# Empty slots of a gathered key list: from row 0 to an index above the gather's bound

## What is computed

```python
def select_keys(scores, q_pos, n_sel):                       # n_sel = 256
    scores = jnp.where(k_pos[None, None, :] <= q_pos[None, :, None], scores, -jnp.inf)
    return lax.top_k(scores, n_sel)[1].astype(jnp.int32)

def sample_attention(q, k_new, v_new, qi, ki_new, wi, cache_k, cache_v, cache_kidx, page_table, rel_bias):
    ...
    idx = select_keys(indexer_scores(qi, wi, ki_all), q_pos, n_sel)
    ...
    def gather(cache, new):
        return jnp.where(in_past[..., None, None], cache[phys, off], gather_rows(new, nidx))
    return sparse_attend(q, gather(cache_k, k_new), gather(cache_v, v_new), q_pos, idx, rel_bias)
```

## Time and profile before

| | |
|---|---|
| median of 3 runs | 1870.47 us (1870.22 to 1871.6) |
| profiled execution, its own time | 1877.6 us |
| span of the profile | 1875.6 us |
| PE, DVE, ACT, POOL busy | 92%, 46%, 35%, 35% |
| DMA packets, bytes | 69477, 158.56 MB |
| gathers of K and V | 256, from 503.4 to 964.1 us |

### The profile page before, as it was taken

How to read it: one execution, slowest core, us unless ns; L and a number is a source line. 1 busy time by engine, 2 the same in 40 slices (tenths; PEclk the granted TensorE clock), 3 DMA queues, 4 the chain that set the end, 5 groups by cost and what they waited for, 6 DMA issues and landing times.

```text
span 1875.6 us, 28975 instructions
## 1 busy us (share of the span) xinstructions
PE 1727.2 (92%) x11176; PEld 1411.4 (75%) x11176; DVE 857.6 (46%) x1809; ACT 653.2 (35%) x1370; POOL 655.2 (35%) x745
## 2 busy tenths in 40 slices
PE   7888999899966787888889999999999999999998
PEld 6553464699944455555555689999999999999997
DVE  4572889277843445666441343313232323232324
ACT  4464787666122333343231022222222121212123
POOL 1100336788554656655513140404040404040300
PEclk9799999999987889999899999999999999999999
DMA  8301202111185656555572001111010102020202
GB/s 241 93 1 48 93 36 77 49 35 42 35 267 147 174 168 180 161 155 157 148 254 81 1 1 45 46 38 53 30 59 22 68 13 76 7 83 2 99 1 96
DMA packets 69477, 158.56 MB, mean 85 GB/s; under 512 B 9402, under 2 KB 26030, under 8 KB 69120
## 3 DMA queue, kind: packets, MB, share of 16 engines
q1 hardware_dynamic: 48000, 85.43, 13.7%
q0 software_dynamic: 21376, 71.75, 12.9%
HBM read 144.40 MB, written 12.76 MB: 84 GB/s over the span
## 4 chain that ended last, share of the span: by engine, by line
PE 82%; DVE 7%; issue 4%; POOL 3%; another core or an unknown queue 2%; ACT 2%; DMA 1%; SPq 0%; DVEq 0%; POOLq 0%; ACTq 0%
PE psum L1841 7%; PE psum L1839 7%; PE psum L1828 7%; PE psum L1827 7%; PE psum L1829 7%; PE psum L1840 7%; PE psum L1768 6%; PE psum L1549 4%; PE psum L1385 3%; PE psum L1398 3%; PE psum L1574 2%; PE psum L1663 2%; PE psum L1685 2%; PE psum L1365 2%
## 5 line engine op out<-in xcount | busy, mean ns | idle before, releaser
L1827 PE MATMUL psum<-n_hi,wup_hi 128*128 128x384 f32 (+1 forms) x768 | 251.3, 327 | 0.0
L1839 PE MATMUL psum<-h_hi,wdn_hi 128*128 128x384 f32 (+1 forms) x768 | 250.9, 327 | 0.0
L1828 PE MATMUL psum<-n_lo,wup_hi 128*128 128x384 f32 (+1 forms) x768 | 250.8, 327 | 0.0
L1829 PE MATMUL psum<-n_hi,wup_lo 128*128 128x384 f32 (+1 forms) x768 | 250.8, 327 | 0.0
L1841 PE MATMUL psum<-h_hi,wdn_lo 128*128 128x384 f32 (+1 forms) x768 | 250.2, 326 | 0.0
L1840 PE MATMUL psum<-h_lo,wdn_hi 128*128 128x384 f32 (+1 forms) x768 | 250.1, 326 | 0.0
L2437 DVE TENSOR_TENSOR h_lo<-h_full,h_hi 128x384 fp32r<-128x384 f32 (+1 forms) x96 | 112.0, 1178 | 262.0 <-ACT h_hi L1246 253.4
L1238 ACT ACTIVATE hrelu<-psum 128x384 f32<-128x384 f32 (+1 forms) x96 | 45.4, 473 | 501.9 <-PE psum L1829 501.9
L932 POOL TENSOR_TENSOR wup_lo<-wup_full,wup_hi 128x4096 fp32r<-128x4096 f32 x8 | 72.3, 9034 | 420.4 <-ACT wup_hi L1222 420.4
L2442 DVE TENSOR_TENSOR x_region<-psum,x_region 128x384 f32<-128x384 f32 (+1 forms) x192 | 102.8, 535 | 252.9 <-PE psum L1841 251.8
L1100 ACT ACTIVATE arena<-x_region,arena 128x384 bf16<-128x384 f32 (+2 forms) x192 | 166.5, 870 | 29.8 <-POOL arena L864 29.8
(11 more groups left out here) (328 smaller groups left out, 3202.0 us busy)
## 6 DMA issues: line engine op xcount, KB each, us to landing
wup_full<-in_w_up SPq DMA_DIRECT2D x8, 2048.0 KB, 8.0
wdn_full<-in_w_down SPq DMA_DIRECT2D x8, 2048.0 KB, 7.7
arena<-in_x_prompt SPq DMA_DIRECT2D x16, 512.0 KB, 9.4
arena<-in_w_in SPq DMA_DIRECT2D x3, 2048.0 KB, 8.4
arena<-in_w_in SPq DMA_DIRECT2D x12, 512.0 KB, 5.7
out<-arena SPq DMA_DIRECT2D x17, 256.0 KB, 4.5
arena<-in_w_out SPq DMA_DIRECT2D x8, 512.0 KB, 9.4
out<-arena SPq DMA_DIRECT2D x8, 512.0 KB, 2.7
```

The lines of the kernel that those rows point to most:

```text
L1827: pe.matmul(b, wu_hi[:, k, col], n_hi[:, k, o:o + w], start=(k == 0), stop=False)
L1828: pe.matmul(b, wu_hi[:, k, col], n_lo[:, k, o:o + w], start=False, stop=False)
L1829: i = pe.matmul(b, wu_lo[:, k, col], n_hi[:, k, o:o + w], start=False, stop=(k == KT - 1))
L1839: pe.matmul(b, wd_hi[:, f, col], h_hi[:, hf, 0:w], start=(f == 0), stop=False)
```

## The change

Every gather of K and V gets a bound, the last row of the cache (40959), and `oob_is_err=False`: a place whose index is above it is passed over, and nothing is copied for it. `slot_lists()` adds 2^20 to the row number of each place that no query wants, so that empty places have such an index. What stays in the ring's empty places is what lay there before; the masks are as they were.

```diff
@@ slot_rows (POOL)
                     pool.indirect_dma_start(ring[:, r % 4, kk, :], None, src,
-                                            bass.IndirectOffsetOnAxis(ap=slotidx[:, c:c + 1], axis=0)).then_inc(ring_in[r % 4], 16)
+                                            bass.IndirectOffsetOnAxis(ap=slotidx[:, c:c + 1], axis=0),
+                                            bounds_check=ck.shape[0] - 1, oob_is_err=False).then_inc(ring_in[r % 4], 16)
@@ slot_lists (VectorE)
-                link(dve.scalar_tensor_tensor(out=sl, in0=bits_[:, 0:128].rearrange("p (b l) -> p b l", b=DB), scalar=256.0,
+                empty, row = (x[:, 0:128].rearrange("p (b l) -> p b l", b=DB) for x in (posi_, hi_))
+                dve.tensor_scalar(empty, got[:, :, 2, :], 0.0, float(1 << 20), ALU.is_equal, ALU.mult)
+                link(dve.scalar_tensor_tensor(out=row, in0=bits_[:, 0:128].rearrange("p (b l) -> p b l", b=DB), scalar=256.0,
                                               in1=got[:, :, 1, :], op0=ALU.mult, op1=ALU.add))
+                link(dve.tensor_tensor(sl, row, empty, ALU.add))
```

## The result

The changed kernel takes 1883.03 us, median of 5 runs (1881.84 to 1888.82), against 1870.54 us for the kernel before (5 runs, 1870.22 to 1871.6). The ratio is 1.0077 [1.0062, 1.0092], so it is slower by 12.5 us. Of these 12.5 us the two profiled executions show only 4.8: that of before was itself 7 us above its median (1877.6 us), that of after is within 1 us of its own (1882.42 us).

The account below looks back on a forecast made before the run. TensorE was busy 92% of the span; in the gathers' stage POOL, not the bytes, set the gathers' pace. Terms -1 + 0.6 + 0.8 = +0.4 us on 1870.47 gave about 1871 us, range 1860 to 1905 us.

Parts of the forecast that it names:

- no change: Whole kernel: the likeliest case, about 1871 us, with 1867 to 1874 us as its range; chance 0.34.
- the smallest difference that can be told: Whole kernel: 0.2%, 3.7 us, taken as about what a measurement can tell from none.
- Bytes: Gathers of K and V: 15.6 MB fall away, worth -1 us, bounds 0 and -3.
- VectorE: Building of the slot list: two more instructions on the path, +0.5 to +0.6 us, taken as +0.6.
- POOL's work in a gather: POOL's time per gather with a bound: taken as 0 us more, range -0.09 to +0.95 us a gather.
- dear end: POOL's gathers: at +0.95 us each, 1973 us or more; a skill-page estimate of 1.3 us a gather would exceed that.
- slower rival: POOL's gathers: dropping rows one by one spends 0.4 us a gather again, about 20 us, 1890 us; chance 0.33.
- the sum's own rule: Gathers' stage: only the 27 gathers under the chain's unattributed pieces, 34 us, count as on the path.
- The register: POOL, ahead of each gather: a 29 ns bound load, 27 on the path, +0.8 us; 7.4 us without cover.
- faster rival: Gathers' stage: TensorE's stalls come from the gathers' traffic and fall with it, about 1863 us; chance 0.30.
- mark: TensorE's "issue" waits in the gathers' stage: near 36 us instead of 47 would show that traffic causes the stalls.

Follow-up runs that it names:

- e3: The changed kernel with the bound at 0, so nearly all rows are passed over; 1789.31 us against 1790.05 for the kernel before, ratio 0.9988.
- e1: The kernel before with only the bound on every gather, all bytes moved; 1791.89 us against 1790.05, ratio 1.0018.
- e6: The kernel before with only the bound on every gather, timed again at the 1871 level; 1885.14 us against 1872.0, ratio 1.0076.
- e5: The changed kernel as it is, timed again at the 1871 level; 1881.12 us against 1872.0 for the kernel before, ratio 1.006.
- e7: The kernel before with 112 rows per gather instead of 128 once the ring is filled, no bound; 1878.4 us against 1872.0, ratio 1.0042.
- e8: The changed kernel with the bound loaded into a register once instead of 256 times; 1871.62 us against 1872.0 for the kernel before, ratio 1.0003.
- e10: The kernel before with the bound from one register loaded once, no VectorE edit, all bytes moved; 1794.61 us against 1788.76, ratio 1.0034.
- e12: The changed kernel with one register load and an empty instruction ahead of each gather; 1874.67 us against 1871.15 for the kernel before, ratio 1.0021.

## Why the prediction was right or wrong

The time lies in the range of 1860 to 1905 us, but that was luck: the range reached beyond 1874 us for a rival, rows handled one by one, that the runs show not to exist. The case that was forecast, no change, is not what happened: the kernel is slower by more than three times what was called the smallest difference that can be told.

*Bytes.* The working gave 15.6 MB, and 15.57 are gone. Their worth was put at -1 us, bounds 0 and -3. The runs agree with a small gain: at the 1790 level all of the gathers' bytes are worth 3 to 5 us (e3 against e1), of which 23%, an estimate in proportion, would be about 1 us. At the 1871 level the bound with all bytes (e6, +13.1 us) and with the 15.6 MB saved (e5, +9.1 us) differ by 4 us, no more than an edit can cost there without adding work (e7). The sentence that the transfers are hidden under POOL's pace held in the main. The Trainium skill, "DMA: Bandwidth & Descriptors", section "The descriptor swizzle", gave 0 for this term; the runs can't tell 0 from 1 us, and they show no partition's engine.

*VectorE.* +0.6 us stood in the sum; two runs give -0.4 and +1.8 us, both within their error of it. The trace of after shows 0.3 us. The term was small and is small.

*POOL's work in a gather.* Taken at 0, with -0.09 to +0.95 us as bounds; it is +0.053 to +0.056 us. The reason given for 0, that the indices are read and turned into addresses either way, was too simple; the reason against a dear end held. The price is the same with no row above the bound (e1), with a quarter (e5), and with nearly all (e3), so the slower rival's mechanism, a second handling row by row, does not exist here. Nor does the dear end that came by the Trainium skill, "GPSIMD Engine Reference", section "Elementwise — side-by-side cycle accounting": 12 cycles an element gave an estimate of 1.3 us a gather, and the runs show 0.05. By the sum's own rule 27 gathers on the path at 0.056 us would be 1.5 us. At the 1871 level e8 shows 0 [-2, +3 us] for it, VectorE's edit and the saved bytes together; its own price there was not measured, and if the 4 us between e5 and e6 are the bytes' worth, it is about as much. At the 1790 level, where POOL has 7% of the chain, e1 and e10 show 2 to 6 us.

*The register: the step that failed.* The prediction put it at +0.8 us, "On the path are the gathers under the unattributed pieces", 27 of them at 29 ns. The duration was right and the pause even hides it. But undoing this one part (e8) takes the change from 1.006 to 1.0003, 9.5 us, and what replaces it in time without being a load (e12) gives back 3.5 us. So at this level a term that was worked out as duration times count was mis-sized by more than ten times, and by its own duration, all 256 on the path, it could be 7.4 us at most. What shows in the profile instead is not POOL: the three profiles with the loads at this level (the change, e5, e6) have 4 to 5% of the chain unattributed and TensorE idle for 102 to 108 us, the four without (before, e7, e8, e12) 1 to 2% and 93 to 95 us. At the 1790 level the loads show no price (e1 against e10), and one and the same kernel, the bound alone, loses 1.8 us there (e1) and 13.1 us here (e6).

*The faster rival and its mark.* It said that TensorE's stalls fall with the bytes, and its mark, "issue" near 36 us, came true in the first profile: 35 us. The time rose all the same, for waits under other names grew by more, those for copies that themselves wait for an unnamed releaser. Nor does the mark go with the bytes: the second profile of the changed kernel has 43.8 us, and the bound alone, with all bytes moved, 38.2. The mark was badly chosen: TensorE's whole idle time in the stage is the thing to compare, and it grew by 7 us, from 94.7 to 101.7.

*What stays open.* Why a register load ahead of each gather lengthens TensorE's stalls, while an instruction of the same length does so less, or not at all; and what these stalls are. All that is shown is that they are in the gathers' stage, that other engines' copies start several us after the last work that the trace has for them to wait for, and that at the 1790 level they are nearly absent. e7 shows that a change with no load and less work can cost 6.4 us at the 1871 level, so a part of the 9.5 us may be the stage's answer to any shift of its timing rather than the loads' own price; e12's 3.5 us point the same way. The loads alone, without a bound, were not tried, nor one register with all bytes at the 1871 level, nor the change at the 1790 level. No version beat the kernel before; the best, e8, equals it.

## What to carry to other kernels

Bytes that pass under another engine's pace are worth little, here some 3 to 5 us of 1790 for all 67 MB; ask what the option that saves them adds to the issuing engine, here 0.05 us on each of 256 gathers. Give a constant bound as a register that is loaded once: at the 1871 level that alone decided between 10 us lost and none, and at the 1790 level no gain from it shows. And when a stage has waits that the profile can't name, count an engine's whole idle time there and not the waits of one name, put no price on an edit by duration times count, and compare only with the kernel before of the same session.

## What the hardware showed that was not expected

- A bound on a gather of 128 rows costs 0.053 us (0.946 to 0.999), whether none or nearly all rows are above it.
- A row that is passed over still leaves a packet. The queue has 20544 packets with 67.16, 51.59 and 0.18 MB; the kernel's packets under 512 B are 13130 with the change and 9402 without it (and with the bound alone). That is 3728 more for the 2 x 3810 rows of K and V that are passed over, about one for two rows. With nearly all of the 2 x 16384 rows passed over (e3) they are 25786, 16384 more, one for two rows again. The share of the DMA engines with nearly all rows passed over is 2.2%, not 0.
- A gather of 112 rows takes 0.925 us, one of 128 rows 0.946: 1.3 ns a row, so by estimate 0.17 us for 128, not the 0.4 us that the prediction put down to the rows.
- One and the same kernel takes 1871 or 1790 us, by the session or the chip: 4.5%, all in the gathers' stage, where TensorE's "issue" waits are 46.9 or 2.4 us.
